# Stage boundaries of a two-block transformer kernel: token tiles staggered in the last group of a product, row chains per tile, the MLP norm applied where the up-products leave PSUM

## What is computed

```
h = rmsnorm(x, mix_pre_gain);  proj = h @ w_in
mixed = concat(attention(proj), recurrence(proj)) @ w_out
x = x + rmsnorm(mixed, mix_post_gain)
h = rmsnorm(x, mlp_pre_gain)
u = relu(h @ w_up);  y = (u * u) @ w_down            # 2048 -> 8192 -> 2048
x = x + rmsnorm(y, mlp_post_gain)
for l in 0, 1:
    shift, scale, gate = split(silu(c) @ ada_w[l] + ada_b[l])
    h = rms_norm(x, norm_g[l]) * (1 + scale) + shift
    z = h @ w_in_2[l];  ...latent attention, convolution...
    x = x + gate * (concat(mla_out, conv_out) @ w_out_2[l])
```

## Time and profile before

| | us |
|---|---|
| time, median of 3 runs | 2126.07 (2123.92 to 2126.21) |
| the profiled execution: its own time | 2126.43 |
| its span, first to last instruction | 2124.5 |
| PE busy | 2037.1 (96%) |
| DVE busy | 1527.5 (72%) |
| ACT busy | 1021.4 (48%) |
| DMA, mean over the span | 207 GB/s |

### The profile page before, as it was taken

The page is one execution under the profiler, slowest core; times in us unless marked ns, Lnnn a source line. Parts: engine busy times, 40 slices in busy tenths (PEclk is TensorE's granted clock), DMA queues, the critical chain, the costliest instruction groups (busy, mean ns, idle before and its releaser), DMA issues.

```text
span 2124.5 us, 31527 instructions
## 1 busy us (share of the span) xinstructions
PE 2037.1 (96%) x13488; PEld 1843.1 (87%) x13488; DVE 1527.5 (72%) x2034; ACT 1021.4 (48%) x1375; POOL 0.2 (0%) x4
## 2 busy tenths in 40 slices
PE   6999998979999999999999889999999899999999
PEld 6999788859999888999888689898998798988887
DVE  4466665677787767778777758989856569888664
ACT  4473754454444333444443464444554555444552
POOL 0000000000000000000000000000000000000000
PEclk9999999989999999999999989999999999999999
DMA  6333334675888888878888824443335344433343
GB/s 241 143 136 120 122 117 159 246 269 200 302 302 314 315 332 319 310 284 328 302 329 321 320 85 154 179 159 124 135 142 195 128 160 176 153 139 120 119 178 119
DMA packets 63356, 440.68 MB, mean 207 GB/s; under 512 B 7153, under 2 KB 7409, under 8 KB 11761
## 3 DMA queue, kind: packets, MB, share of 16 engines
q1 hardware_dynamic: 61776, 434.91, 55.7%
q10 hardware_dynamic: 1440, 3.76, 0.5%
HBM read 436.55 MB, written 2.10 MB: 206 GB/s over the span
## 4 chain that ended last, share of the span: by engine, by line
PE 88%; DVE 8%; ACT 3%; issue 1%; DMA 1%; DVEq 0%; SPq 0%; ACTq 0%
PE PS L455 16%; PE PS L456 15%; PE PS L457 15%; PE PS L466 11%; PE PS L467 11%; PE PS L468 11%; PE PS L432 8%; DVE WL L859 2%; DVE UG L1197 2%; ACT WH L1546 1%; DVE Y L904 1%; DVE X L1399 0%; PE PS L486 0%; DMA X<-in_x 0%; ACT S L1602 0%
## 5 line engine op out<-in xcount | busy, mean ns | idle before, releaser
L859 DVE TENSOR_TENSOR WL<-RAW,WH 128x1024 fp32r<-128x1024 f32 (+1 forms) x636 | 763.8, 1209 | 481.8 <-ACT WH L1546 481.1
L1546 ACT ACTIVATE WH<-RAW 128x1024 fp32r<-128x1024 f32 (+1 forms) x636 | 659.9, 1046 | 843.1 <-PE PS L457 507.6
L455 PE MATMUL PS<-HTh,WH 128*128 128x256 f32 x2928 | 848.2, 290 | 11.1 <-DVE HTl L911 4.4
L456 PE MATMUL PS<-HTl,WH 128*128 128x256 f32 x2928 | 833.7, 285 | 0.0
L457 PE MATMUL PS<-HTh,WL 128*128 128x256 f32 x2928 | 833.5, 285 | 0.0
L455 PEld LDWEIGHTS PS<-HTh,WH 128*128 128x128 f32 x2928 | 566.7, 194 | 34.8 <-issue 25.3
L456 PEld LDWEIGHTS PS<-HTl,WH 128*128 128x128 f32 x2928 | 567.1, 194 | 0.4
L457 PEld LDWEIGHTS PS<-HTh,WL 128*128 128x128 f32 x2928 | 566.7, 194 | 0.0
L868 DVE SCALAR_TENSOR_TENSOR RAW<-RAW,CB 128x2048 f32<-128x2048 f32 x96 | 219.3, 2285 | 3.1 <-ACT CB L1980 3.1
L467 PE MATMUL PS<-WL,Uh 128*128 128x512 f32 x512 | 202.9, 396 | 0.0
L466 PE MATMUL PS<-WH,Uh 128*128 128x512 f32 x512 | 202.1, 395 | 0.2 <-DVE WL L859 0.2
(11 more groups left out here) (269 smaller groups left out, 1669.9 us busy)
## 6 DMA issues: line engine op xcount, KB each, us to landing
RAW<-in_w_in SPq DMA_DIRECT2D x112, 1024.0 KB, 4.8
RAW<-in_ada_w SPq DMA_DIRECT2D x96, 1024.0 KB, 5.6
RAW<-in_w_up SPq DMA_DIRECT2D x64, 1024.0 KB, 5.5
RAW<-in_w_down SPq DMA_DIRECT2D x64, 1024.0 KB, 5.4
RAW<-in_w_out SPq DMA_DIRECT2D x48, 1024.0 KB, 4.8
RAW<-in_w_pw SPq DMA_DIRECT2D x8, 1024.0 KB, 4.8
RAW<-in_w_in SPq DMA_DIRECT2D x8, 768.0 KB, 4.1
RAW<-in_w_q_up SPq DMA_DIRECT2D x6, 1024.0 KB, 4.8
```

What stands on the lines that cost most here:

```text
L455: e.matmul(out, sh, ah, start=first and i % 2 == 0, stop=False, skip_group_check=True)
L456: e.matmul(out, sh, al, start=False, stop=False, skip_group_check=True)
L859: e.tensor_tensor(m[f"WL{j % NHL}"][:, 0:nk * w], m[f"RAW{i % NRAW}"][:, k0 * w:(k0 + nk) * w], m[f"WH{j % NHL}"][:, 0:nk * w].bitcast(F32 ...
L1546: e.activation(m[f"WH{j % NHL}"][:, 0:nk * w], m[f"RAW{i % NRAW}"][:, k0 * w:(k0 + nk) * w], ACT.Copy).then_inc(signals["high"], 1)
```

## The change

- **Staggered last group.** In w_out 3, w_down 7 and w_out2 3 of each layer, PE computes token tile 0 one half ahead of token tile 1, so tile 0 is complete two half-tiles before the group's end and says so with a semaphore (tile0). During the last two halves of such a group nothing is cut ahead; those splits come after the first and second beat of the turn.
- **Row chains per tile.** Squares, mean, root, reciprocal, update of X and scaling are done for each tile by itself, X in pieces of 128x512. Squares are taken from PSUM in the first block's mixer (its copy to Y goes), a square root is called early so that its table is loaded before it is needed, and `gates` (L1459 before) is moved ahead of the last group.
- **MLP norm.** X itself is transposed after w_out; its squares are taken during the turn, the factor of each token is spread over partitions by two small matmuls (x_wide) into a row XR, and DVE applies it with the relu as the up-products leave PSUM. ACT then squares and copies, DVE subtracts.
- **Order of the rest.** `rope_tables` starts after w_up 0 rather than with the turn. The 8 first chunks of ada_w stand among the 8 chunks of w_out 1 and 2, one behind each; w_out 3, w_up 0 and w_down 7 have none, so 88 stand among 116 chunks (88 among 128 before).
- **Start.** The two tiles of x come on two queues, DVE squares one and ACT the other; two of the four scaled pieces per tile are made before the first weights are split.

```diff
-            self.cut_ahead()
+            if not (n.staggered and j >= n.done - 2):
+                self.cut_ahead()
...
-    spread(ADA_OUT, ("w_out", range(1, 4)))
-    spread(len(adaptive), ("w_up", range(8)), ("w_down", range(4)), ("w_up", range(8, 16)),
-           ("w_down", range(4, 8)))
+    spread(ADA_OUT, ("w_out", range(1, 3)))
+    weights("w_out", (3,))
+    weights("w_up", (0,))
+    spread(len(adaptive), ("w_up", range(1, 8)), ("w_down", range(4)), ("w_up", range(8, 16)),
+           ("w_down", range(4, 7)))
+    weights("w_down", (7,))
...
+        def tile(j, nk, tt):
+            for kk in range(nk):
+                kt = 2 * (j - n.first) + kk
+                op = row_products(bk, None, (0, n.width), tt, act_h(kt), act_l(kt), m[f"WH{j % NHL}"],
+                                  m[f"WL{j % NHL}"], kk * n.width, kt == 0, kt == n.kts - 1)
+            return op
+
+        for j, nk in course.begin(n):
+            pe.wait_ge("split", j + 1)
+            for kk in range(nk):
+                pe.wait_ge(*ready(2 * (j - n.first) + kk))
+            op = tile(j, nk, 0)
+            if j == n.done - 1:
+                op.then_inc(signals["tile0"], 1)
+            if j > n.first:
+                tile(j - 1, 2, 1).then_inc(signals["half_done"], 1)
+        tile(j, nk, 1).then_inc(signals["half_done"], 1)
...
+            if q == 1:
+                pe.wait_ge("x_up", TURNED_BY[q][kt // 4])
+            else:
+                pe.wait_ge("xs", 8 * (q - (q > 1)) + TURNED_BY[q][kt // 4])
             for tt in range(2):
-                op = e.transpose(bank[b][:, 128 * tt:128 * tt + 128], Y[:, tt, 128 * kt:128 * kt + 128], ident)
+                op = e.transpose(bank[b][:, 128 * tt:128 * tt + 128],
+                                 m["X" if q == 1 else "Y"][:, tt, 128 * kt:128 * kt + 128], ident)
...
+            b = small()
+            pe.wait_ge("rstd", 4)
+            for tt in range(2):
+                op = mm(b, 128 * tt, 128 * tt + 128, m["ST"][:, 54 + tt:55 + tt].broadcast_to([128, 128]), ident,
+                        tt == 0, tt == 1)
+            op.then_inc(signals["x_wide"], 1)
...
+    def row_norm(r, n, i):
+
+        mean_square(42 + i, 1, 32 + 4 * i, 4, 2048.0, "y_sq", 8 * r + 6 + i + 1)
+        gained(r, n, 3, i)
+        row_rstd(42 + i)
+        dve.wait_ge("y_gain", 8 * r + 6 + i + 1)
+
+    def updated(i, *cs):
+        for c in cs:
+            x, y = X[:, i, 512 * c:512 * c + 512], Y[:, i, 512 * c:512 * c + 512]
+            e.scalar_tensor_tensor(x, y, ST[:, 42 + i:43 + i], x, ALU.mult, ALU.add).then_inc(signals["x_up"], 1)
...
+    mean_square(54, 2, 44, 1, 2048.0, "x_sq", 2)
+    row_rstd(54, 2)
+    for c in range(2):
+        scaled(0, c)
+        scaled(1, c)
...
+        row_norm(0, n, i)
+        updated(i, 0, 1, 2, 3)
...
+    course.cut_ahead(1)
+    course.beat()
+    course.cut_ahead()
     for half in range(2):
         for g in range(8):
-            course.group(group["w_up", 8 * half + g])
+            n = group["w_up", 8 * half + g]
+            course.group(n)
+            if half == 0 and g == 0:
+                course.start(rope_tables())
+                dve.wait_ge("x_wide", 1)
+                e.tensor_copy(m["XR"][:, :], wide[0][:, 0:256]).then_inc(signals["x_row"], 1)
+                dve.wait_ge("x_row", 1)
+            dve.wait_ge("half_done", n.done)
+            for i in range(2):
+                e.scalar_tensor_tensor(VT[:, 2 * i:2 * i + 2, :],
+                                       bank[2 * n.pair + i][:, :].rearrange("p (a b) -> p a b", a=2), 0.0,
+                                       bc_tok(m["XR"][:, :], 2), ALU.max, ALU.mult).then_inc(signals["up_relu"], 1)
...
+    dve.wait_ge("tile0", 2)
+    sums(n, 3, 0)
+    row_norm(1, n, 0)
+    updated(0, 0)
+    dve.wait_ge("half_done", n.done)
+    sums(n, 3, 1)
+    updated(0, 1, 2, 3)
+    row_norm(1, n, 1)
+    updated(1, 0, 1)
+    mean_square(54, 1, 44, 4, 2048.0, "x_sq", 14)
+    updated(1, 2, 3)
+    row_rstd(54)
+    scaled(0, 0, 1)
+    mean_square(55, 1, 48, 4, 2048.0, "x_sq", 18)
+    row_rstd(55)
+    scaled(1, 0, 1)
+    for c in range(2, 4):
+        scaled(0, c)
+        scaled(1, c)
...
+                    mean_square(54 + i, 1, 44 + 4 * i, 4, 2048.0, "x_sq", 18 + 7 + i)
+                    row_rstd(54 + i)
+                    scaled(i, 0, 1, 2, 3)
...
+    e.dma_start(X[:, 1, :], t["x"][0, 128:256, :]).then_inc(signals["x1"], 16)
+    e.dma_start(m["CN"][:, 0:128], t["cn"][:, 0:128]).then_inc(signals["id"], 16)
     e.dma_start(m["PK"][:, :], t["pk"]).then_inc(signals["pk"], 16)
-    e.dma_start(m["CN"][:, 0:128], t["cn"][:, 0:128]).then_inc(signals["id"], 16)
-    for tt in range(2):
-        act.wait_ge(f"x{tt}", 16)
-        e.activation(Y[:, tt, :], X[:, tt, :], ACT.Square, accum_out=ST[:, 44 + tt:45 + tt]).then_inc(
-            signals["x_sq"], 1)
+    act.wait_ge("warm", 1)
+    root_table()
+    act.wait_ge("x1", 16)
+    e.activation(Y[:, 1, :], X[:, 1, :], ACT.Square, accum_out=ST[:, 45:46]).then_inc(signals["x_sq"], 1)
+    row_root(54, 2)
```

More of the change, by code:

```diff
@@ L146, in beat, with cut_ahead @@
                     break
-    def cut_ahead(self):
-        while self.opened < len(self.chunks):
+    def cut_ahead(self, most=99):
+        while self.opened < len(self.chunks) and most:
             if self.chunks[self.opened][0] == "a":
@@ L156, in cut_ahead @@
                 self.cut += 1
+                most -= 1
             else:
@@ L267, in weight_course @@
                 mark = ("stored", stored)
-        n = Group(first, count, k0, kts, w, pair, mark, None if k0 else before.get(pair))
+        staggered = (tensor, g) in (("w_out", 3), ("w_down", 7)) or (tensor[:6] == "w_out2" and g == 3)
+        n = Group(first, count, k0, kts, w, pair, mark, None if k0 else before.get(pair), staggered)
         before[pair] = mark
@@ L347, in tiles @@
         sb(c, "Ul", [128, 32, 256], F32R)
+        sb(c, "XR", [128, 256])
     with ExitStack() as c:
@@ L432, in mm, with row_products, staggered @@
         return e.matmul(bank[b][rows, c0:c1], lhs, rhs, start=st, stop=sp, skip_group_check=True)
+    def row_products(bk, cols, rows, tt, ah, al, wh, wl, at, first, final):
+        c, width = rows
+        sh, sl = ah[:, 128 * tt:128 * tt + 128], al[:, 128 * tt:128 * tt + 128]
+        mh, ml = wh[:, at + c:at + c + width], wl[:, at + c:at + c + width]
+        out = bk[1][:, width * tt:width * tt + width] if cols else bk[tt][:, 0:width]
+        st = first and not (cols and tt)
+        e.matmul(out, sh, mh, start=st, stop=False, skip_group_check=True)
+        e.matmul(out, sh, ml, start=False, stop=False, skip_group_check=True)
+        return e.matmul(out, sl, mh, start=False, stop=final, skip_group_check=True)
+    def staggered(n, act_h, act_l, ready):
+        if n.before:
+            pe.wait_ge(*n.before)
+        if n.pair >= 2:
+            for b in (2 * n.pair, 2 * n.pair + 1):
+                pe.wait_ge(*free[b])
+        bk = [bank[2 * n.pair], bank[2 * n.pair + 1]]
+        def tile(j, nk, tt):
[14 more added lines that the diff above has]
+        tile(j, nk, 1).then_inc(signals["half_done"], 1)
+        if n.pair >= 2:
+            free[2 * n.pair] = free[2 * n.pair + 1] = n.taken
     def products(n, act_h, act_l, ready, cols=None, rows=None):
@@ L788, in tensor_program @@
     course.drain(side_a, side_r, side_h)
-    for cg in range(4):
-        products(group["w_out", cg], *hidden, lambda kt: ("mix_l", kt // 4 + 1), rows=(0, 512))
+    mixed = lambda kt: ("mix_l", kt // 4 + 1)
+    for cg in range(3):
+        products(group["w_out", cg], *hidden, mixed, rows=(0, 512))
+    staggered(group["w_out", 3], *hidden, mixed)
     course.start(turn(1))
+    course.cut_ahead()
     course.beat(2)
-    course.start(rope_tables())
     h = h_ready(1)
     for half in range(2):
+        ready = lambda kt: ("up_l", 16 * half + kt // 2 + 1)
         for g in range(8):
             products(group["w_up", 8 * half + g], *hidden, h, cols=4)
-        for cg in range(4):
-            products(group["w_down", 4 * half + cg], tile_of("Uh"), tile_of("Ul"),
-                     lambda kt: ("up_l", 16 * half + kt // 2 + 1), rows=(0, 512))
+            if half == 0 and g == 0:
+                course.start(rope_tables())
+        for cg in range(3 if half else 4):
+            products(group["w_down", 4 * half + cg], tile_of("Uh"), tile_of("Ul"), ready, rows=(0, 512))
+    staggered(group["w_down", 7], tile_of("Uh"), tile_of("Ul"), ready)
     for L in range(2):
         course.start(turn(2 + L))
+        course.cut_ahead()
         course.beat(2)
@@ L835, in tensor_program @@
                      lambda kt: ("p_l", 8 * L + kt // 2 + 1), cols=4)
[L836 to L840 removed]
+        both = (lambda kt: m["OH"][:, kt, :] if kt < 8 else HTh[:, kt - 8, :],
+                lambda kt: m["OL"][:, kt, :] if kt < 8 else HTl[:, kt - 8, :],
```

(18 more changed lines are left out.)

291 lines of the change are left out of this document (169 added, 122 removed).

## The result

| | before | changed |
|---|---|---|
| median of the runs, us | 2126.14 | 2103.93 |
| lowest to highest, us (4 runs each) | 2123.92 to 2130.27 | 2101.84 to 2105.94 |
| profiled execution: time, span, us | 2126.43, 2124.5 | 2105.94, 2104.2 |
| PE busy, us | 2037.1 | 2036.7 |
| span minus PE busy, us | 87.4 | 67.5 |

What follows compares the result with a forecast made beforehand. PE bounds the kernel: its work plus its waits, 87 us. From 2126.4 us, gains of 26.4 less new waits of 4.3 and 6.1 gave 2110.4, taken as 2110, range 2101 to 2117.

Steps and rivals of the forecast that it cites:

- case A: Whole kernel: the forecast itself, 2104 to 2115 us by its bounds; chance 0.55.
- After w_out: Boundary behind w_out: transposes of X 4.2 us behind the last product's end instead of 14.46, gain 10.3 us (9 to 11.4).
- silu(c): First ada_w chunk, w_out 1: DVE waits for ACT's silu, PE waits 2.6 us plus 1.7 half clock: loss 4.3 (2 to 6).
- Case B: Neither new queue stalls PE, the silu being earlier or the positions there in time: 2100 us; chance 0.17.
- case C: Transfers of weights and ada_w bound w_out 1 and 2: 2115 us; chance 0.14.
- Turn and rope tables: Steps leaving the turn after w_out gain 7.0 us; behind w_up 0 they cost 6.1, 4.4 of it PE's wait.
- After w_down: Boundary behind w_down: chain stays in series, transposes 12 us behind the last product's end instead of 14.67, gain 2.7 (1.5 to 4).
- Start: Kernel start: table load ahead of data, four scalings before HTl; first product at 15.2 instead of 18.19, gain 2.9 (1.8 to 4.2).
- Between the layers and the tail: Layer boundary: transposes about 6.2 us behind the last product's end, gain 2.2 (1.5 to 3); kernel end: gain 1.3 (0.6 to 1.4).
- The drain of 1.38 us: Skill's rule for every table switch: three hidden loads would give 1.38 us more each, sum 4.1 lower; left out.
- D: Boundary chains shrink less, 2 to 3 us more at each of three boundaries: 2117 us; chance 0.09.
- E: Rival: hand-over after 15 later up groups exceeds its 1.5 us margin, 2143 us, chance 0.05. In E+ times: boundary's last product's end.

## Why the prediction was right, and where its terms were off

The sum forecast 16.0 us less than the profiled execution before; it was 20.3. The median, 2103.93 us, lies in the range, at the lower edge of case A (2104 to 2115). Of the 4.3 us between the two, by the table of events, 2.1 are after w_down, 0.9 at the start, 0.7 after w_out, 1.8 in the two stretches that the change does not touch, and the turn with the rope tables took back 1.1. Term by term:

- **After w_out: right.** 10.3 forecast for the transposes, 10.6 measured (14.46 to 3.84). The chain of the changed kernel has the two rows of four updates in 2.74 us each, as worked out:

```profile
457.65 2.74 DVE X L1489 x4
...
461.35 2.74 DVE X L1489 x4
```

Three of the experiments, each undoing one part, cost 4.1 us here for the splits left out, about 5 for the norm put off, 1.2 for the stagger. They come near 10.6 together but leave nothing for the chunk of ada_w that also went, so the split between the parts is rough.
- **silu(c): right.** Forecast a wait of 2.6 and 4.3 us in all; measured 2.37 and 4.3 between the two events of the table, 1.7 of it half clock behind the wait. The experiment with silu(c) earlier shows the cause. Case B, in which neither wait comes, is out, and so is case C.
- **Turn and rope tables: wait right, balance off.** Forecast a wait of 4.4 us in w_up 1, measured 4.52. The positions took 3.8 us to land, not 3.1 to 3.4. The two gave together +0.9 in the sum and were -0.2 (idle time 0.8 more, half clock 0.7 less from the first product of w_up 0 to the end of w_down), because the turn before cost less than the 7.0 that I put in: 3.5 us of waits and 12.51 x (1 - 0.79) = 2.6 of clock in the 16 us around them (first row below, before), while the new wait cost 4.5 and 2.4 of clock (second row, changed).

```profile
488.00:504.00 16.00, 12.51 (x78) 12.33 (x79) 13.25 (x22) 7.11 (x12) 0.00 (x0) 0.79 0.53 198
```

```profile
500.00:516.00 16.00, 11.48 (x81) 11.28 (x80) 12.39 (x24) 6.21 (x8) 0.00 (x0) 0.79 0.25 92
```

- **After w_down: mechanism right, size off, the largest miss.** I put the transposes at E+12, they came at E+10.23, 1.8 us sooner (the gain was 4.4 where I had 2.7). The step that failed is the sum of the serial chain: "with 0.03 to 0.05 of issue for some 25 steps". The chain of the changed kernel there:

```profile
1204.26 0.75 DVE X L1489
1205.01 0.60 DVE Y L920
1205.61 1.99 DVE X L1489 x3
...
1208.56 1.41 DVE X L1489 x2
...
1210.30 1.32 DVE X L1489 x2
1211.62 0.09 DVE ST L968
...
1211.73 0.88 DVE Y L973 x2
...
1212.90 0.21 ACT ST L1713
```

The eight updates are priced rightly (5.47 us for 8 x 0.69), and the first of them ends at E+1.4 for E+1.5. After that the chain gains 0.35 us on my count until tile 1's gain, another 0.5 at the last mean and root, which end at E+9.7 and not at E+10.5 (means and reciprocals add 0.08 or 0.09 us each in several places, where I took up to 0.2), and nearly the whole 1.0 us for issue: the chain has 0.02 or 0.03 us of it at a step and 0.14 ahead of the first transposes, some 0.4 us in all.

- **Start: right cause, 0.9 too small.** 3.8 us instead of 2.9. Of the bounds I gave, the upper one was nearer, since x landed 1.1 us earlier. The experiment shows that the two queues did it, and not PK, which I had named.
- **Between the layers and the tail: right**, 2.0 and 1.3 for 2.2 and 1.3. The drain of 1.38 us for each table load, which the prediction names and leaves out, is not what made the sum too small: in all three chains before, the load starts 0.02 us after the squares end and the root 0.01 us after the load, and with the drain the gain between the layers would have been 3.6 us.
- **Not in the sum: the clock.** 1.1 us were gained before w_out 0 and 0.7 in the first layer, where the change does nothing. The first is the half clock at 352 us, shown above, that the changed kernel's first profile lacks and its second has; in the first layer half clock cost 2.4 us before and 1.6 after. Such stretches come and go by 2 us either way, which is the size of my miss on several terms; 20.3 is therefore not known better than to 2 us.

Of the rivals, D (chains that shrink less) went the other way after w_down and within 0.3 us of the forecast elsewhere, and E (a slower way out of the up groups) did not occur: PE waits in none of the 15 later up groups.

## What to carry to other kernels

Before shortening a chain between two stages, look at what stands ahead of it in the queues of its engines: two weight splits left out of the last halves were worth 12 us, the early tile 2. When work is moved, ask of each instruction in it what input it needs and which engine issues the transfer; both new waits were an instruction at the head of an in-order queue whose input another engine produced late, and both went, one by making the input earlier, the other by that and smaller pieces. Count waits in full. The half clock behind the two waits went with them, but other stretches of half clock come and go between executions by as much, so look for it at the place of the wait and not in the time of a few runs. And list everything that stands in a chain before: the chunk of ada_w in the one after w_out, 2.2 us, left it unnoticed.

## What I had not expected of the hardware

The half clock does not belong to waits alone. Twelve profiles lose 16.7 to 20.5 us to it, whether PE waits 60 or 87 us. Waits of 2.4 us in w_out 1 had it behind them nine times out of nine, waits of 2.0, 0.7 and 0.2 us in w_up 1 had none, and with a PE that was busy throughout it stood at 352 us, behind eight narrow products, in one execution and not in another of the same kernel. Nor had I expected row steps of one column to be so cheap in a chain: the timeline gives 0.15 to 0.17 us for one, but where it starts before the instruction ahead of it has ended it adds only 0.08 or 0.09, by the rows after w_down.
